# A decoder kernel's expert sums: one head's copies and scores, and the next head's query halves, one group of rows later

## The reference

```python
def peer_layer(h, w_q, sub_keys, u_tab, v_tab):
    q = (hf @ w_q).reshape(T, 8, 2, 128)
    s = jnp.einsum('thpd,hpnd->thpn', q, sub_keys)
    sc, idx = lax.top_k(s, 16)
    cand = sc[:, :, 0, :, None] + sc[:, :, 1, None, :]
    cidx = idx[:, :, 0, :, None] * 128 + idx[:, :, 1, None, :]
    top_sc, pos = lax.top_k(cand, 16)
    eidx = jnp.take_along_axis(cidx, pos, axis=-1)
    gate = jax.nn.softmax(top_sc, axis=-1)
    act = gelu(jnp.einsum('thkd,td->thk', u_tab[eidx], hf))
    return jnp.einsum('thk,thkd->td', gate * act, v_tab[eidx])
```

## Time and profile before

| | us |
|---|---|
| median of 3 runs | 1602.05 |
| lowest, highest | 1601.07, 1605.98 |
| profiled execution, its time | 1602.66 |
| profiled execution, its span | 1600.6 |
| TensorE busy in the span | 1482.5 (93%) |
| VectorE busy | 1058.9 (66%) |
| ScalarE busy | 551.5 (34%) |
| POOL busy | 569.2 (36%) |
| DMA over the span | 571.91 MB, 357 GB/s |

### The profile page before, as it was taken

How to read it: one execution, slowest core, us unless ns; L and a number is a source line. 1 busy time by engine, 2 the same in 40 slices (tenths; PEclk the granted TensorE clock), 3 DMA queues, 4 the chain that set the end, 5 groups by cost and what they waited for, 6 DMA issues and landing times.

```text
span 1600.6 us, 22838 instructions
## 1 busy us (share of the span) xinstructions
PE 1482.5 (93%) x8300; PEld 1139.6 (71%) x8300; DVE 1058.9 (66%) x2176; ACT 551.5 (34%) x1145; POOL 569.2 (36%) x383
## 2 busy tenths in 40 slices
PE   8999999999999999999999998898989897778787
PEld 7999997767999999998989995444444343333333
DVE  6655386755744328998984658785858585858556
ACT  6444363454544436443116343221212121212113
POOL 2555437110244441001001324454545444544451
PEclk9999999999999999999999999999999999999898
DMA  9888958994999997998956859999999999999996
GB/s 363 317 321 327 351 212 338 312 327 150 384 373 374 367 386 283 370 399 340 363 221 238 347 208 381 419 428 426 427 427 427 426 427 427 427 427 426 427 427 271
DMA packets 99814, 571.91 MB, mean 357 GB/s; under 512 B 11536, under 2 KB 11664, under 8 KB 50448
## 3 DMA queue, kind: packets, MB, share of 16 engines
q1 hardware_dynamic: 61056, 298.15, 50.2%
q0 software_dynamic: 37520, 268.47, 40.0%
q10 hardware_dynamic: 1152, 4.16, 0.7%
HBM read 569.67 MB, written 135.27 MB: 440 GB/s over the span
## 4 chain that ended last, share of the span: by engine, by line
PE 60%; DMA 21%; DVE 12%; issue 2%; POOL 2%; ACT 2%; ACTq 0%; DVEq 0%; POOLq 0%
DMA arena<-pairs,eidx 15%; PE ps L2705 12%; PE ps L2093 8%; PE ps L2091 8%; PE ps L2092 8%; DMA ring<-pairs,eidx 6%; DVE arena L1616 3%; PE ps L2180 2%; PE ps L2178 2%; PE ps L2179 2%; PE ps L2431 2%; PE ps L2482 1%; POOL w_lo L733 1%; PE ps L2596 1%; PE ps L2668 1%
## 5 line engine op out<-in xcount | busy, mean ns | idle before, releaser
L2705 PE MATMUL ps<-arena 128*128 128x512 f32 x912 | 431.1, 627 | 82.6 <-ACT arena L1235 82.6
L2705 PEld LDWEIGHTS ps<-arena 128*128 128x128 f32 x912 | 178.5, 200 | 321.0 <-issue 208.5
L1945 DVE CUSTOM_DVE_ANT_0 arena<-arena 128x1024 f32<-128x1024 f32 x228 | 275.3, 1223 | 158.8 <-DMA arena<-pairs,eidx 158.7
L800 POOL DMA_INDIRECT arena<-pairs,eidx x227 | 270.2, 1191 | 286.0 <-PE ps L2705 244.0
L733 POOL TENSOR_TENSOR w_lo<-ring,w_hi 128x1024 fp32r<-128x1024 f32 x76 | 208.2, 2741 | 259.1 <-DVE w_lo L1288 175.2
L2091 PE MATMUL ps<-u_hi,w_hi 128*128 128x256 f32 (+1 forms) x912 | 259.5, 285 | 3.6 <-POOL w_lo L733 2.4
L2093 PE MATMUL ps<-u_hi,w_lo 128*128 128x256 f32 (+1 forms) x912 | 259.5, 285 | 0.0
L2092 PE MATMUL ps<-u_lo,w_hi 128*128 128x256 f32 (+1 forms) x912 | 259.2, 284 | 0.0
L820 ACT ACTIVATE w_hi<-ring 128x1024 fp32r<-128x1024 f32 x188 | 197.7, 1056 | 149.1 <-PE ps L2180 71.2
L2091 PEld LDWEIGHTS ps<-u_hi,w_hi 128*128 128x128 f32 x912 | 172.1, 189 | 5.4 <-issue 2.5
L2093 PEld LDWEIGHTS ps<-u_hi,w_lo 128*128 128x128 f32 x912 | 172.3, 189 | 0.0
(11 more groups left out here) (392 smaller groups left out, 2465.2 us busy)
## 6 DMA issues: line engine op xcount, KB each, us to landing
ring<-in_stream SPq DMA_DIRECT2D x121, 1024.0 KB, 7.0
pairs<-in_peer_u SPq DMA_DIRECT2D x128, 512.0 KB, 7.6
pairs<-in_peer_v SPq DMA_DIRECT2D x128, 512.0 KB, 8.8
arena<-in_ada SPq DMA_DIRECT2D x32, 768.0 KB, 6.3
arena<-in_stream SPq DMA_DIRECT2D x8, 1024.0 KB, 10.2
arena<-pairs,eidx POOLq DMA_INDIRECT x227, 17.9
h<-in_x_t SPq DMA_DIRECT2D x2, 544.0 KB, 5.1
ring<-in_stream SPq DMA_DIRECT2D x2, 512.0 KB, 6.8
```

Source lines behind the costliest of these rows:

```text
L800: pool.indirect_dma_start(slot_of(n), None, pairs, own).then_inc(landing(n)[0], 16)
L1945: dve.tensor_tensor_reduce(row, row, hf[:, n % HEAD_ROWS // TOPK, :], 1.0, 0.0, ALU.mult, ALU.add, dots[:, n % HEAD_ROWS:n % HEAD_ROWS + 1 ...
L2705: mm = pe.matmul(ps[:, Y_BANKS[j // TOPK] + half, :], diag[:, n % DIAGS, :], slot_of(n)[:, D + half * 512:D + half * 512 + 512], start=(hd ...
```

## The change

Three edits. ScalarE does `half_head(1, 0)`, `half_head(1, 1)` and `score_copy(1)` behind the diagonals of group 1 instead of group 0. TensorE makes `all_scores(1)` ahead of group 2 instead of group 1. And the two halves of head 2's query, on TensorE and ScalarE, go one group later each: on TensorE from ahead of group 2 and group 4 to ahead of group 3 and group 5; the scores of head 2 follow one group behind the second half, as before, so from group 5 to group 6.

```diff
-HALF_HEADS = {1: (2, 0), 3: (2, 1), 5: (3, 0), 7: (3, 1), 10: (4, 0), 13: (4, 1),
+HALF_HEADS = {2: (2, 0), 4: (2, 1), 5: (3, 0), 7: (3, 1), 10: (4, 0), 13: (4, 1),
               16: (5, 0), 19: (5, 1), 22: (6, 0), 25: (6, 1), 28: (7, 0), 31: (7, 1)}
...
                 if g == 0:
                     for n in range(2, 2 * TT):
                         tok_copy(n)
+                if g == 1:
                     for e in range(2):
                         half_head(1, e)
                     score_copy(1)
-                if g == 1:
                     first_gate_exp(1)
...
                 if g == 1:
                     for e in range(2):
                         next_query(1, e)
+                if g == 2:
                     all_scores(1)
                 if g - 1 in HALF_HEADS:
                     half_head(*HALF_HEADS[g - 1])
```

## The result

Over 8 runs each, the changed kernel took 1614.10 us (1610.74 to 1618.19), the kernel before 1604.38 (1601.07 to 1607.56). The ratio is 1.0064, 95% interval 1.0050 to 1.0078: +10.3 us (8.0 to 12.5) where +6.0 was forecast, and 1614.1 lies above the range. The profiled execution took 1613.49 us, its span is 1611.4.

What follows compares the result with a forecast made beforehand. Gathers of expert rows, 2.46 us each, were taken to bound the kernel. Terms 0 + 5.5 (row 25) + 0.5 (refill) gave +6.0 us: 1608.7 from the profiled 1602.66, 1608.1 against the median 1602.05; range 1604.5 to 1610.5.

Steps and rivals of the forecast that it cites:

- The sign: Whole kernel: slower, with chance 0.74; same 0.24, faster 0.02.
- main term: Row 25's gather, waiting for head 2's second half behind group 4, lands 5.5 us later, into an empty queue.
- the refill: Rows behind row 25, gathered into an empty queue, lose 0.5 us against the full rate, out of 0 to 1.3.
- Step 1: Group 1: ScalarE's gelu no longer waits behind head 1's copies; sums start 3.1 us earlier, row 16 gains 0.3 us.
- Step 2: ScalarE's score copy in group 1 waits for TensorE, delaying exp and gate_made; group 2's sums start only 0.8 us earlier.
- Step 3: Head 2's first half goes behind group 2; group 3's sums start 2.0 us later, at 999.6, hidden by the queue.
- Step 4: Row 25's gather waits for head 2's second half, now behind group 4; issued at 1018.6, it lands 5.5 us later.
- Step 5: The rest: head 2's scores move to group 6, later slots keep their place, later issues shift alike; cost 0.
- the premise: From the 980 us stretch on, a gather landing x us later moves the end by x, nothing behind having slack.
- A: Rival: group 4 is summed early enough that row 25's issue leaves no hole; 0 to -2.2 us, chance 0.07.
- B: Rival: rows 17 to 19 issue earlier and lose less, so row 25's hole is smaller; +2 to +4.8, chance 0.17.
- C: Rival: rows 26 to 29 are issued slowly, every 2.7 us at worst; +7.6 to +9 us, chance 0.08.

Runs made afterwards that it cites:

- e6: The change plus 40 unused score matmuls on TensorE ahead of group 2's sums; 1.0043 against the kernel before, +6.9 us.
- e2: The kernel before with only head 2's halves moved one group later, head 1's copies and scores kept in place; 1.0059 against the kernel before, +9.5 us.
- e3: The change, but head 2's first half stays ahead of group 2, so only its second half is late; 1.0055 against the kernel before, +8.8 us.
- e9: e3 plus 32 unused score matmuls on TensorE ahead of group 4's sums; 1.0043 against the kernel before, +6.9 us.
- e5: The change, but head 2's weight slot is first reused at row 30 instead of row 25; 1.0018 against the kernel before, +2.9 us.
- e10: Kernel before with head 1's copies and scores moved, exp before score copy, head 2's halves ahead of group 2, slot 8 from row 17; 0.9995, -0.8 us.
- e7: The change with both e5's slot at row 30 and e6's unused matmuls; 1.0002 against the kernel before, +0.3 us.

## Why the prediction was wrong

The sign, the place and the mechanism of the main term were right; a second cost was missed, in a step that I had costed by the wrong duration, and two smaller terms, group 4's start and the refill, were mis-sized.

- **Step 1** held. The gelu of group 1 ran at 973.76 less 2.8 = 970.9 (forecast 971.9), and group 1's sums started at 975.3, as forecast.
- **Step 2** held. gate_made started at 985.4 (985.6), waiting for the exp, and group 2's sums at 988.9 (989.2).
- **Step 3 failed.** I wrote that head 2's first half "lay in a gap" and moved it out at no other cost, and gave group 2's sums 7.0 us. It was this half that kept the gap short. The gap stood in my own numbers: head 1's scores done at 983.5, group 2's sums from 989.2, 5.7 us with nothing between, and I put no price on it. TensorE idled 5.75 us, its clock fell to the lower level, and the sums took 9.95 us. Group 3 started at 1002.2 instead of the forecast 999.6. The gathers of rows 17 to 20, each waiting for one of group 2's rows, went out 0.8 to 1.8 us late, the dots of rows 18 to 23 started 2.2 to 3.1 us late, and group 4, which waits for row 19, started at 1010.7 instead of 1007.8. e6 puts a price on this: 2.1 us of the whole by the profiled executions, 3.4 by the ratios, whose intervals overlap.
- **Step 4** held in kind: POOL idled 11.19 us on the half head, rows 26 to 29 behind it. Its issue missed the forecast by 3.0 us (1021.6 against 1018.6). In e6, where group 2 is fast, it came at 1021.85 (2.2 us are scatter there, since group 1 starts 0.6 us earlier than in the change), so at 1019.6: 2.0 of the 3.0 us came in through step 3. The other 1.0 is group 4, which started at 1010.99 less 2.2 = 1008.8 in e6: I had passed 0.8 us of group 2's lead on to it, and row 19's dot started no earlier than before (+0.2). Row 25's own time to its dot was 5.5 us, 0.4 less than the 5.9 that I took.
- **The refill** was under-sized: row 26's dot started 3.44 us behind row 25's though it was issued 1.3 us behind it, 1.0 us above the steady 2.46; I had taken 0.5. e2 and e3 have 3.40 and 3.45 here, e6 and e9, with the filler, 2.55 and 2.57 and a later loss instead (by row 34 e6 has lost 1.3 us more than at row 27). What sets it stays open.
- **The sum** with measured terms: row 25's dot waited for its landing until 1029.96 less 2.8 = 1027.1, against a landing at 1019.0 before: +8.1. With 1.0 for the refill +9.1, which is row 27's +9.1 in the table, and +8.8 at the end. The runs say +10.3 (8.0 to 12.5); the 1.5 us between are within that interval and not explained.
- **Step 5 and the premise.** From row 27 to the end the change loses nothing more (9.1, then 8.8), as step 5 had it. That a gather landing x us later moves the end by x held here to 0.3 us, but only within 2 us in the other versions of the table.
- **The rivals.** A (the cover holds) was wrong; what it asked for, a row 25 that doesn't wait, is e5. B (a smaller hole) was wrong: rows 17 to 19 went out later, not earlier. C put the extra on slow issues, but POOL took 0.93 to 1.47 us for rows 25 to 29, so that isn't it, though its price was near.
- **The range** was too narrow because all of its cases took the 16 matmuls of a group at 7.1 us. The kernel before shows another duration behind the stretch that I worked with. TensorE, groups 6, 7 and 10 of the kernel before, and two later ones:

```profile
1028.16 7.13 PE L2705 MATMUL ps<-arena 128*128 128x512 f32 x16 [1.19 <-ACT arena L1235]
1038.09 8.83 PE L2705 MATMUL ps<-arena 128*128 128x512 f32 x16 [2.80 <-ACT arena L1235]
...
1068.04 7.13 PE L2705 MATMUL ps<-arena 128*128 128x512 f32 x16 [3.04 <-ACT arena L1235]
...
1246.55 8.83 PE L2705 MATMUL ps<-arena 128*128 128x512 f32 x16 [3.86 <-ACT arena L1235]
...
1405.23 8.57 PE L2705 MATMUL ps<-arena 128*128 128x512 f32 x16 [4.60 <-ACT arena L1235]
```

Behind 2.80 us of idle the same 16 matmuls took 8.83 us, behind 3.04 us 7.13: gaps of that length may or may not cost 1.7 us. But all four groups behind 3.4 us or more in the kernel before took 8.57 to 9.86 us. Those were the rows to price a new gap of 5.7 us by: 1.4 to 2.7 us on group 2, and a range that reaches higher by as much. Even 1610.5 plus 2.7 is 1613.2, below the measured 1614.1. A part of the miss lies in the base: the forecast and the range stood on 1602.05, the median of three runs, and over eight runs the kernel before has 1604.38. That is 2.3 of the 6.0 us between 1608.1 and 1614.1, and chance.

## What to carry to other kernels

Work that sits in an idle stretch of TensorE isn't free to move: before moving it, write down how long the engine will stand still without it, and look in the trace for what the same matmuls take behind such a gap. Where a buffer is released by a step, the step's due time is that of the gather that waits for it, and in-order issue puts everything behind that gather into the same delay; moving the buffer's first use back by five rows cured 7 us here. And once the queue that sets the time had run dry, nothing behind it gave the time back here.

## What the runs showed of the hardware

- Idle stretches of 4.37, 4.67 and 5.75 us ahead of a group went with 8.83, 8.83 and 9.40 to 9.96 us for 16 matmuls that take 7.13 otherwise. Counted over the expert layer in all 12 profiled executions, for groups with all 16 matmuls in the trace: behind 1.9 us of idle or less, none of 440 took over 7.14 us; behind 3.69 us or more, each of 49 took 8.5 to 10.2; between these, 124 of 271 took under 7.2 us and the others up to 10.2 (7.13 behind 3.61 in e10, 8.83 behind 2.29 in e9). What decides in between, and why the longer gaps cost 1.7 in one place and 2.8 in another, was not tried.
- The kernel before has such slow groups too, as the 8.83 us at 1038.09, while 428 GB/s were moved from 1036 to 1050, the full rate. There the slow sums took nothing from the rate of the gathers; group 2's came where rows 17 to 20 waited for them.
- Added matmuls without any use (5.5 us in all with head 1's scores) took about 2 us off the changed kernel by the profiled executions (e6), and 2.4 us off the median of e5 (e7).
- A gather issued into an empty queue took 5.4 to 6.0 us from issue to the start of its dot (row 25 in the change, e2, e3, e6 and e9), and the one behind it came 3.4 us later in three of them and 2.6 in two, not 2.46.
